# A hybrid decoder layer on one core: sliding-window scores and value products of two heads joined on halves of the TensorE array

## The chip, the cores and the metric

The kernel runs on one core of a Trainium2 chip. The metric is the device time of one execution in microseconds, as the median of repeated runs.

## The reference

One decoder layer over 2048 tokens of width 1024, all in float32. A mixer (four HGRN2 heads beside eight sliding-window query heads), then cross attention over 256 memory tokens, then an MLP. The change touches only the sliding-window group:

```
q: 8 heads x 64, k and v: 2 heads x 64 (4 query heads share one key head)
q, k = partial_rope(head_rms(.))           # per head
query block n (128 rows) reads key blocks n-1 and n (256 keys), causal, window 128
s = q k^T / 8;  m = max(max(s), sink);  p = exp(s - m)
o = (p / (sum(p) + exp(sink - m))) v       # (128 rows x 64) per head and block
```

## The kernel before

**Staging.** The mixer works through the sequence in four blocks of 512 tokens (`TB`), everything with the feature on the partitions and the token along the free axis. In each block, 22 projection panels (128 output features) are multiplied in three products of split operands (lines 1560, 1563 and 1570), each panel as the steps `("make", n, part)`, and each is copied out by ScalarE in the step `take`. Beside them run the HGRN2 heads 0 to 3 (`hg_...`, `gate_...`, `spans_...`) and the sliding attention of the head pairs t = 0 to 3.

**Order.** All engines follow one list of steps written out by hand (`mixer_steps`, woven by `weave` with `PLACES`): each engine issues its own part of a step, in the order of the list, and waits on semaphores (`Signal.at`). For the attention of a pair the list is made by `attend(t)`. A pair has two heads of 64 features that lie on partitions 0 to 63 and 64 to 127 of `qk`. It has four sub-steps q = 0 to 3, numbered through a block by a = 4t + q: q = 0 and 1 are the even and the odd head of query tiles 0 and 1, q = 2 and 3 the even and the odd head of tiles 2 and 3. The list runs them as a pipeline of four stages:

```
for n in range(QT + 3):
    scores(n);  scale(n-1) + turn(n-2);  pv(n-3)     # each if its number is 0 to 3
```

- `scores` (TensorE, line 1703): two matmuls of 128 queries by 256 keys into one of three banks. The stationary operand is all 128 partitions of `qk`, both heads; the other head's half of the moving `kpad` holds zeros. `kpad` has four planes: key head times even or odd. VectorE adds the window and takes the maximum (line 1502, into `s_sb`, three places), ScalarE takes the exponential (line 1244) and the sink's (line 1248).
- `scale` (VectorE, lines 1514 to 1519): the denominators, and two multiplications.
- `turn` (TensorE, line 1714): four transposes of 128x128 into the bank `TURN`; it waits until ScalarE has emptied `TURN` of the sub-step before. ScalarE copies `TURN` to `pT` (line 1256), which has two places.
- `pv` (TensorE, line 1726): four matmuls with the 128x64 values as stationary operand and 128 columns of `pT`, into the 64 partitions of the bank `OUT` that belong to the even or the odd head.

Behind the last `pv`, the step `hg_transpose` of the next head (lines 1612 and 1617) waits for the last copy of `TURN`, and `att_out` copies `OUT` (line 1262). The steps `hg_scores` (line 1643: seven levels, two output halves of 64 partitions in turn, 64 columns each) and `hg_delta` (line 1626: eight matmuls of 128 columns with 64 partitions of contraction each, the two halves of the partitions in turn, into two banks) belong to the HGRN2 heads.

**Keys.** `sw_keys` multiplies the rotated keys by duplicating matrices (lines 1690, 1691), and ScalarE copies them in four pieces of 64 partitions to the planes of `kpad` (line 1236); the rotation of the first pair (line 1686) waits for these copies, since it writes the bank `ROT`. VectorE moves the last key tile to the front for the next block (line 1458). `kpad` is cleared once, at the start (line 1327). The squares of the next block's norm use the first two places of `pT` as their buffer (`sq`).

Of the kernel before, what the change touches and what calls it, by code (L numbers as in the profile page):

```python
# [23 lines left out]
ACT = mybir.ActivationFunctionType  # L24
AX = mybir.AxisListType

P = 128
# [5 lines left out]
TB = 512  # L33
NBLK = SEQ // TB
QT = TB // P
# [722 lines left out]
def mixer(nc, block, sems, sh, xT, w_mix, rope_d, y_d, w_cross, lows_d):  # L758
# [17 lines left out]
    with ExitStack() as ctx:  # L776
# [45 lines left out]
        tn = sb("tn", [P, 2, TB])  # L822
        tcos = sb("tcos", [P, TB])
        qk = sb("qk", [P, 2, TB])
        kpad = sb("kpad", [P, 4, P + TB])
        vsw = sb("vsw", [P, 1 + QT, P])
        s_sb = sb("s_sb", [P, 3, 2, 2 * P])
        pT = sb("pT", [P, 2, TB])
        sq = pT
        stat = sb("stat", [P, 3, 5, 2])  # L830
        small = sb("small", [P, 3, 2 * QT])
# [238 lines left out]
        def _(act):  # L1070
# [80 lines left out]
            def turn(blk, steps):  # L1151
                for step in steps:
# [76 lines left out]
                    elif kind == "sw_keys":  # L1229
                        act.wait_ge(k_old.sem, k_old.at(blk, 0))  # L1230
                        for kv in range(2):
                            done = (k_dup0, k_dup1)[kv]
                            act.wait_ge(done.sem, done.at(blk, 0))
                            for n in range(2):
                                rows = slice(n * SW_D, (n + 1) * SW_D)
                                last = act.activation(kpad[rows, 2 * kv + n, P:], (TURN, ROT)[kv][rows, :], ACT.Copy)
                            last.then_inc((k_ok0, k_ok1)[kv].sem, 1)
                    elif kind == "scores":
                        a = step[1]
                        t, q = ATT[a]  # L1240
# [9 lines left out]
                    elif kind == "turn":  # L1250
                        a = step[1]
                        act.wait_ge(a_tr.sem, a_tr.at(blk, a))
                        act.wait_ge(a_o.sem, a_o.at(blk, a - 2))
                        if ATT[a][0] == 1 and has_next(blk):
                            act.wait_ge(n_sum.sem, n_sum.at(blk, KT - 1))
                        act.activation(pT[:, a % 2, :], TURN[:], ACT.Copy).then_inc(a_pt.sem, 1)
                    elif kind == "att_out":
                        t = step[1]
                        act.wait_ge(a_o.sem, a_o.at(blk, (t + 1) * QT - 1))
                        out = stored[3 if t == SW_PAIRS - 1 else 1]  # L1260
                        act.wait_ge(out.sem, out.at(blk, -1))
                        act.activation(yT[:, HEADS + t, :], OUT[:], ACT.Copy).then_inc(y_att.sem, 1)
                        if t == SW_PAIRS - 1:
                            out = block_of(y_d, blk)
                            act.wait_ge(y_hg.sem, y_hg.at(blk, HEADS - 1))
                            act.dma_start(out[:, HEADS - 1, :], yT[:, HEADS - 1, :]).then_inc(stored[2].sem, 16)
                            act.wait_ge(y_att.sem, y_att.at(blk, t))
                            act.dma_start(out[:, KT - 1, :], yT[:, KT - 1, :]).then_inc(stored[3].sem, 16)
# [11 lines left out]
        def _(dve):  # L1280
# [42 lines left out]
                                  ALU.mult).then_inc(p_ok.sem, 1)  # L1323

            dve.wait_ge(sh["kept"], 48)
            for t in (state[:], kpad[:], vsw[:, QT, :], vtok[:], rope[:, 1, :]):
                dve.memset(t, 0.0).then_inc(set_up, 1)
            dve.memset(rope[:, 0, :], 1.0).then_inc(set_up, 1)
            dve.wait_ge(set_up, 6)
# [1 line left out]
            def turn(blk, steps):  # L1331
                for step in steps:
# [118 lines left out]
                    elif kind == "sw_values":  # L1451
# [3 lines left out]
                        dve.wait_ge(v_ok.sem, v_ok.at(blk, -1))  # L1455
                        dve.tensor_copy(vsw[:, 0, :], vsw[:, QT, :]).then_inc(v_old.sem, 1)
                        dve.wait_ge(k_ok1.sem, k_ok1.at(blk, -1))
                        dve.tensor_copy(kpad[:, :, 0:P], kpad[:, :, TB:]).then_inc(k_old.sem, 1)
                    elif kind == "sw_root":

                        n = step[1]
# [68 lines left out]
        def _(pe):  # L1530
# [65 lines left out]
            def turn(blk, steps):  # L1596
                for step in steps:
# [94 lines left out]
                    elif kind == "scores":  # L1692
                        a = step[1]
                        t, q = ATT[a]
                        if q == 0:

                            pe.wait_ge(h_pr.sem, h_pr.at(blk, (t + 1) * NCH // 2 - 1))
                            pe.wait_ge(s_qk.sem, s_qk.at(blk, 1 + t))
                        if q >= 3:
                            pe.wait_ge(a_s.sem, a_s.at(blk, a - 3))  # L1700
                        for i in range(2):
                            tq = q // 2 * 2 + i
                            last = pe.matmul(SCORE[a % 3][:, i * 2 * P:(i + 1) * 2 * P],  # L1703
                                             qk[:, t % 2, tq * P:(tq + 1) * P],
                                             kpad[:, t // 2 * 2 + q % 2, tq * P:(tq + 2) * P], start=True, stop=True)
                        last.then_inc(a_sc.sem, 1)
                    elif kind == "turn":
                        a = step[1]
                        pe.wait_ge(a_pn.sem, a_pn.at(blk, a))
# [7 lines left out]
                    elif kind == "pv":  # L1717
                        a = step[1]
                        t, q = ATT[a]
                        if q == 0:  # L1720
                            pe.wait_ge(h_y.sem, h_y.at(blk, t))
                        pe.wait_ge(a_pt.sem, a_pt.at(blk, a))
                        for i in range(2):
                            tq = q // 2 * 2 + i
                            for kt in range(2):
                                last = pe.matmul(OUT[q % 2 * SW_D:(q % 2 + 1) * SW_D, tq * P:(tq + 1) * P],  # L1726
                                                 vsw[:, tq + kt, t // 2 * SW_D:(t // 2 + 1) * SW_D],
                                                 pT[:, a % 2, (2 * kt + i) * P:(2 * kt + i + 1) * P],
                                                 start=kt == 0, stop=kt == 1)
                        last.then_inc(a_o.sem, 1)  # L1730

            pe.wait_ge(s_xhi, KT)
            pe.wait_ge(s_xln, 4 + KT)
# [1606 lines left out]
```

## Time and profile before

| | |
|---|---|
| median of 3 runs | 2691.37 us (2687.94 to 2693.91) |
| the profiled execution's own time | 2685.68 us |
| its span from first to last instruction | 2683.9 us |
| TensorE busy | 2594.5 us, 97% |
| VectorE busy | 1731.4 us, 65% |
| ScalarE busy | 1145.2 us, 43% |
| the mixer | from about 84 to 976 us of the span |

Times are microseconds. A float32 matmul is recorded as two instructions. A matmul's recorded duration holds the time to fill and drain the array, so the pace of a group is read from the chain or from the starts, not from the mean. "[0.77 <-ACT ktok L1214]" means that the engine had been idle for 0.77 us and what ended it.

### The profile page before, as it was taken

How to read it: one execution, taken by the hardware profiler on the slowest of the kernel's cores; microseconds unless marked ns; L12 is line 12 of the kernel's file. 1: busy time of each engine (PE TensorE's matmuls, PEld its weight loads, DVE VectorE, ACT ScalarE, POOL GpSimd, SP SyncE). 2: the span in 40 equal slices, each digit the busy share in tenths (PEclk: the TensorE clock that was granted, in tenths of full speed). 3: DMA queues.
4: the chain of work that ended last, by engine and by line, in shares of the span. 5: the costliest groups of instructions: out<-in, count | busy, mean ns of one | idle time of the engine just before them, and what ended most of it. 6: DMA issues, size and time to landing. Idle time of an engine off the chain costs nothing.

```text
span 2683.9 us, 39324 instructions
## 1 busy us (share of the span) xinstructions
PE 2594.5 (97%) x13654; PEld 2110.1 (79%) x13654; DVE 1731.4 (65%) x3010; ACT 1145.2 (43%) x2179; POOL 896.4 (33%) x1018
## 2 busy tenths in 40 slices
PE   7999999999999989999998999999999999999999
PEld 5777777777777878877786888888888888888887
DVE  6678567756756656575657586687666354556665
ACT  5455455555445545654565332252223233332231
POOL 1332100000000037336535576747666222222222
PEclk9999999999999999999999999999999999999999
DMA  4432532343243343145315234423334963444664
GB/s 181 144 111 80 184 103 95 113 165 95 94 168 106 104 176 130 52 166 196 115 51 195 95 126 153 142 98 122 124 121 138 325 176 102 137 138 142 208 186 146
DMA packets 184509, 369.17 MB, mean 138 GB/s; under 512 B 13168, under 2 KB 79088, under 8 KB 181616
## 3 DMA queue, kind: packets, MB, share of 16 engines
q1 hardware_dynamic: 179152, 357.08, 39.9%
q10 hardware_dynamic: 5152, 9.51, 1.0%
q8 instruction: 110, 1.80, 0.3%
q14 instruction: 95, 0.78, 0.1%
HBM read 286.71 MB, written 79.82 MB: 137 GB/s over the span
## 4 chain that ended last, share of the span: by engine, by line
PE 78%; DVE 9%; ACT 5%; issue 4%; DMA 2%; POOL 2%; ACTq 0%; DVEq 0%; SPq 0%; POOLq 0%
PE bank L3256 8%; PE bank L3254 8%; PE bank L3258 8%; PE bank L3234 6%; PE bank L3230 6%; PE bank L3231 6%; PE bank L1570 5%; PE bank L1560 5%; PE bank L1563 5%; PE bank L2184 2%; PE bank L2179 2%; PE bank L2180 2%; PE bank L1726 2%; PE bank L1643 2%; PE bank L1703 2%
## 5 line engine op out<-in xcount | busy, mean ns | idle before, releaser
L478 POOL TENSOR_TENSOR wlo<-raw,whi 128x256 fp32r<-128x256 f32 x372 | 321.1, 894 | 1119.0 <-ACT whi L1162 641.9
L1560 PE MATMUL bank<-hi,whi 128*128 128x512 f32 x704 | 297.4, 422 | 2.0 <-ACT whi L1158 1.9
L1563 PE MATMUL bank<-lo,whi 128*128 128x512 f32 x704 | 279.9, 398 | 4.7 <-DVE lo L1314 4.7
L3256 PE MATMUL bank<-lo,whi 128*128 128x512 f32 x896 | 275.8, 389 | 0.0
L3254 PE MATMUL bank<-hi,whi 128*128 128x512 f32 x896 | 275.8, 389 | 0.0
L3258 PE MATMUL bank<-hi,wlo 128*128 128x512 f32 x896 | 275.8, 389 | 0.0
L3046 DVE TENSOR_TENSOR lo<-h,hi 128x1024 fp32r<-128x1024 f32 x80 | 124.5, 1556 | 172.8 <-ACT hi L2810 172.8
L2741 POOL TENSOR_TENSOR wlo<-h,whi 128x256 fp32r<-128x256 f32 x160 | 127.8, 823 | 298.3 <-ACT whi L2802 298.3
L2179 PE MATMUL bank<-hi,whi 128*128 128x512 f32 x504 | 208.6, 414 | 10.5 <-DVE h L2072 6.5
L2180 PE MATMUL bank<-lo,whi 128*128 128x512 f32 x504 | 197.8, 393 | 0.0
L3258 PEld LDWEIGHTS bank<-hi,wlo 128*128 128x128 f32 x896 | 168.2, 188 | 34.9
L3256 PEld LDWEIGHTS bank<-lo,whi 128*128 128x128 f32 x896 | 168.2, 188 | 34.9
L3254 PEld LDWEIGHTS bank<-hi,whi 128*128 128x128 f32 x896 | 168.2, 188 | 34.9
L2723 POOL TENSOR_TENSOR wlo<-raw,whi 128x256 fp32r<-128x256 f32 x166 | 151.1, 936 | 122.2 <-ACT whi L2751 120.0
L1570 PE MATMUL bank<-hi,wlo 128*128 128x512 f32 x704 | 189.9, 412 | 0.0
L2802 ACT ACTIVATE whi<-h 128x512 fp32r<-128x512 f32 x80 | 50.6, 632 | 289.1 <-PE bank L3258 271.4
L1563 PEld LDWEIGHTS bank<-lo,whi 128*128 128x128 f32 x704 | 134.3, 191 | 38.7 <-DVE lo L1314 9.4
L2723 POOL TENSOR_TENSOR m_xlo<-raw,m_xhi 128x256 fp32r<-128x256 f32 x174 | 163.6, 973 | 0.0
L1560 PEld LDWEIGHTS bank<-hi,whi 128*128 128x128 f32 x704 | 134.3, 191 | 34.7 <-issue 7.0
L1570 PEld LDWEIGHTS bank<-hi,wlo 128*128 128x128 f32 x704 | 130.8, 190 | 35.0 <-issue 9.6
L2751 ACT ACTIVATE whi<-raw 128x512 fp32r<-128x512 f32 x87 | 54.5, 629 | 228.2 <-DMA raw<-w_mlp 184.6
L3230 PE MATMUL bank<-hi,whi 128*128 128x512 f32 x348 | 136.0, 391 | 1.1 <-issue 0.6
(395 smaller groups left out, 5804.9 us busy)
## 6 DMA issues: line engine op xcount, KB each, us to landing
h<-hidden_scratch SPq DMA_DIRECT2D x96, 512.0 KB, 4.3
raw<-w_mix SPq DMA_DIRECT2D x88, 512.0 KB, 4.1
raw<-w_cross SPq DMA_DIRECT2D x64, 512.0 KB, 3.4
raw<-w_mlp SPq DMA_DIRECT2D x64, 512.0 KB, 4.6
wlo<-mixer_lows_scratch SPq DMA_DIRECT2D x60, 512.0 KB, 3.5
hidden_scratch<-hT SPq DMA_DIRECT2D x116, 256.0 KB, 2.0
h<-w_mlp SPq DMA_DIRECT2D x112, 256.0 KB, 3.0
mixer_lows_scratch<-wlo SPq DMA_DIRECT2D x22, 512.0 KB, 2.9
```

Source lines behind the costliest of these rows:

```text
L478: last = pool.tensor_tensor(wlo[:, i, cols], raw[:, i, cols], whi[:, i, cols].bitcast(F32), ALU.subtract)
L1560: pe.matmul(out, w, hi[:, k, :], start=k == 0, stop=False)
L1563: pe.matmul(out, w, lo[:, k, :], start=False, stop=False)
L1570: last = pe.matmul(out, wlo[:, i % 2, k * P:(k + 1) * P], hi[:, k, :], start=False, stop=k == KT - 1)
L2179: pe.matmul(out, w, hi[b][:, k, :], start=k == 0, stop=False)
L2180: pe.matmul(out, w, lo[b][:, k, :], start=False, stop=False)
L2723: last = pool.tensor_tensor(lo_tile[:, cols], source(half, n, w)[:, cols], hi_tile[:, cols].bitcast(F32), ALU.subtract)
L3230: pe.matmul(acc, hi_tile[:, cols], parts(half, m, k)[0], start=k == 0, stop=False)
L3231: pe.matmul(acc, hi_tile[:, cols], parts(half, m, k)[1], start=False, stop=False)
L3254: pe.matmul(down_bank(i)[:], wh[:, cols], xh[:, i % 2, :], start=K == 0, stop=False)
L3256: pe.matmul(down_bank(i)[:], wh[:, cols], xl[:, i % 2, :], start=False, stop=False)
L3258: last = pe.matmul(down_bank(i)[:], wl[:, cols], xh[:, i % 2, :], start=False, stop=K == KD - 1)
```

## The change

The two heads of a pair are computed together. `kpad` (four planes with zeros in one half) becomes `ksw` (two planes, both halves filled), copied by one 128-partition instruction for each key head. The score matmuls of q = 0 and 1, and those of q = 2 and 3, are issued together at the place of the even one, each with 64 partitions of contraction, and the even and odd head alternate. The value products of a pair of sub-steps are issued together at the place of the odd one, with the two output halves alternating. `pT` has four places, and the copy into it waits for the value product four sub-steps back.

```diff
-        kpad = sb("kpad", [P, 4, P + TB])
+        ksw = sb("ksw", [P, 2, P + TB])
-        pT = sb("pT", [P, 2, TB])
+        pT = sb("pT", [P, QT, TB])
...
-                            for n in range(2):
-                                rows = slice(n * SW_D, (n + 1) * SW_D)
-                                last = act.activation(kpad[rows, 2 * kv + n, P:], (TURN, ROT)[kv][rows, :], ACT.Copy)
-                            last.then_inc((k_ok0, k_ok1)[kv].sem, 1)
+                            act.activation(ksw[:, kv, P:], (TURN, ROT)[kv][:], ACT.Copy).then_inc((k_ok0, k_ok1)[kv].sem, 1)
...
-                        act.wait_ge(a_o.sem, a_o.at(blk, a - 2))
+                        act.wait_ge(a_o.sem, a_o.at(blk, a - QT))
-                        act.activation(pT[:, a % 2, :], TURN[:], ACT.Copy).then_inc(a_pt.sem, 1)
+                        act.activation(pT[:, a % QT, :], TURN[:], ACT.Copy).then_inc(a_pt.sem, 1)
...
-                        dve.tensor_copy(kpad[:, :, 0:P], kpad[:, :, TB:]).then_inc(k_old.sem, 1)
+                        dve.tensor_copy(ksw[:, :, 0:P], ksw[:, :, TB:]).then_inc(k_old.sem, 1)
...
                     elif kind == "scores":
+                        if q % 2:
+                            continue
                         if q == 0:
...
-                        if q >= 3:
-                            pe.wait_ge(a_s.sem, a_s.at(blk, a - 3))
+                        else:
+                            pe.wait_ge(a_s.sem, a_s.at(blk, a - 2))
                         for i in range(2):
-                            tq = q // 2 * 2 + i
-                            last = pe.matmul(SCORE[a % 3][:, i * 2 * P:(i + 1) * 2 * P],
-                                             qk[:, t % 2, tq * P:(tq + 1) * P],
-                                             kpad[:, t // 2 * 2 + q % 2, tq * P:(tq + 2) * P], start=True, stop=True)
-                        last.then_inc(a_sc.sem, 1)
+                            for odd in range(2):
+                                rows = slice(odd * SW_D, (odd + 1) * SW_D)
+                                last = pe.matmul(SCORE[(a + odd) % 3][:, i * 2 * P:(i + 1) * 2 * P],
+                                                 qk[rows, t % 2, (q + i) * P:(q + i + 1) * P],
+                                                 ksw[rows, t // 2, (q + i) * P:(q + i + 2) * P], start=True, stop=True)
+                                if i:
+                                    last.then_inc(a_sc.sem, 1)
...
                     elif kind == "pv":
-                        if q == 0:
+                        if q % 2 == 0:
+                            continue
+                        if q == 1:
                             pe.wait_ge(h_y.sem, h_y.at(blk, t))
                         pe.wait_ge(a_pt.sem, a_pt.at(blk, a))
-                        for i in range(2):
-                            tq = q // 2 * 2 + i
+                        for tq in (q - 1, q):
                             for kt in range(2):
-                                last = pe.matmul(OUT[q % 2 * SW_D:(q % 2 + 1) * SW_D, tq * P:(tq + 1) * P],
-                                                 vsw[:, tq + kt, t // 2 * SW_D:(t // 2 + 1) * SW_D],
-                                                 pT[:, a % 2, (2 * kt + i) * P:(2 * kt + i + 1) * P],
-                                                 start=kt == 0, stop=kt == 1)
-                        last.then_inc(a_o.sem, 1)
+                                for odd in range(2):
+                                    last = pe.matmul(OUT[odd * SW_D:(odd + 1) * SW_D, tq * P:(tq + 1) * P],
+                                                     vsw[:, tq + kt, t // 2 * SW_D:(t // 2 + 1) * SW_D],
+                                                     pT[:, q - 1 + odd, (2 * kt + tq - q + 1) * P:(2 * kt + tq - q + 2) * P],
+                                                     start=kt == 0, stop=kt == 1)
+                                    if tq == q and kt:
+                                        last.then_inc(a_o.sem, 1)
```

## Rows read from the trace of the kernel before

**Rows 1.** The page: the span, and part 1, busy time of each engine.

```profile
span 2683.9 us, 39324 instructions
PE 2594.5 (97%) x13654; PEld 2110.1 (79%) x13654; DVE 1731.4 (65%) x3010; ACT 1145.2 (43%) x2179; POOL 896.4 (33%) x1018
```

**Rows 2.** Stretch 84 to 976: PE, PEld, DVE, ACT, POOL busy; clock, DMA.

```profile
84.00:976.00 892.00, 852.97 (x5960) 685.60 (x5959) 599.94 (x1565) 465.97 (x1016) 75.78 (x96) 0.98 0.35 119
```

**Rows 3.** The chain that ended last, 84 to 976: shares by line.

```profile
by line: PE bank L1570 15.9%; PE bank L1560 14.7%; PE bank L1563 14.4%; PE bank L1726 6.1%; PE bank L1643 5.4%; issue 5.3%; PE bank L1703 5.2%; PE bank L1714 3.2%; PE bank L1656 2.4%; PE bank L1657 2.1%; DVE lo L1314 1.8%; PE bank L1686 1.6
```

**Rows 4.** Groups of TensorE instructions by line, 84 to 976.

```profile
L1703 PE MATMUL bank<-kpad,qk 128*128 128x256 f32 x256 | 65.9, 380 | 1.3 <-DVE qk L1491 1.3
L1726 PE MATMUL bank<-pT,vsw 128*64 128x128 f32 x511 | 64.2, 279 | 0.0
```

**Rows 5.** The chain in order of time (start, length), pair 0 of block 1.

```profile
367.32 0.87 PE bank L1703 x4
...
372.26 1.02 PE bank L1726 x8
373.28 0.43 PE bank L1560
...
373.94 0.24 PE bank L1560
...
379.26 1.77 PE bank L1726 x16
381.04 0.59 PE bank L1612 x4
```

**Rows 6.** The chain in order of time: `hg_scores` and `hg_delta` of head 2.

```profile
437.47 1.78 PE bank L1643 x56
...
443.11 1.09 PE bank L1626 x16
```

**Rows 7.** Timeline: the last `turn` of pair 0, and `hg_delta` of head 3.

```profile
378.66 0.60 PE L1714 MATMUL bank<-con,s_sb 128*128 128x128 f32 x4
...
379.30 0.60 ACT L1256 ACTIVATE pT<-bank 128x512 f32<-128x512 f32 x1 [2.29 <-PE bank L1714]
...
487.11 0.60 ACT L1214 ACTIVATE ktok<-bank 128x512 f32<-128x512 f32 x1
...
487.86 1.16 PE L1626 MATMUL bank<-vtok,ktok 64*128 64x128 f32 x16 [0.77 <-ACT ktok L1214]
```

**Rows 8.** Timeline: TensorE's wait in pair 1; pair 2 before its second `turn`.

```profile
413.04 1.10 PE L1536 MATMUL bank<-sqsum,con 128*128 128x512 f32 x2 [1.97 <-ACT nguess L1085]
...
475.42 0.58 ACT L1256 ACTIVATE pT<-bank 128x512 f32<-128x512 f32 x1
...
476.80 0.60 PE L1714 MATMUL bank<-con,s_sb 128*128 128x128 f32 x4
```

**Rows 9.** Timeline: the keys of block 1 and the first scores.

```profile
350.93 2.40 ACT L1236 ACTIVATE kpad<-bank 64x512 f32<-64x512 f32 x4
351.06 0.69 DVE L1286 TENSOR_TENSOR rstd<-rstd,mean 128x512 f32<-128x512 f32 x1 [3.83 <-ACT rstd L1114]
...
353.38 1.12 PE L1686 MATMUL bank<-tn,rotq 128*128 128x512 f32 x2 [1.14 <-ACT kpad L1236]
...
356.71 1.10 PE L1703 MATMUL bank<-kpad,qk 128*128 128x256 f32 x4 [0.37 <-DVE qk L1491]
```

**Rows 10.** Timeline: the clearing of `kpad`, and TensorE's first wait behind it.

```profile
58.02 2.19 DVE L1327 MEMSET kpad<- 128x2560 f32 x1 [0.48 <-ACT fg L1125]
...
80.64 1.08 PE L1617 MATMUL bank<-con,kend 128*128 128x128 f32 x4 [2.77 <-ACT qdec L1193]
```

**Rows 11.** Who waited for whom, 84 to 976: total, times, longest.

```profile
DVE prod L1438 <- PE bank L1643: 73.1, 29, 8.1
DVE s_sb L1502 <- PE bank L1703: 18.7, 13, 1.9
```

**Rows 12.** Two stretches, columns as in the stretch of Rows 2.

```profile
405.00:420.00 15.00, 13.04 (x55) 9.88 (x54) 12.50 (x36) 10.80 (x24) 0.00 (x0) 1.00 0.26 75
490.00:505.00 15.00, 12.18 (x90) 8.59 (x90) 11.81 (x26) 3.59 (x9) 0.00 (x0) 0.77 0.12 37
```

More of the change, by code:

```diff
@@ L1325, in _ @@
             dve.wait_ge(sh["kept"], 48)
-            for t in (state[:], kpad[:], vsw[:, QT, :], vtok[:], rope[:, 1, :]):
+            for t in (state[:], ksw[:], vsw[:, QT, :], vtok[:], rope[:, 1, :]):
                 dve.memset(t, 0.0).then_inc(set_up, 1)
```

## The prediction

> **What bounds the kernel now.** The page comes first: TensorE is busy for 97% of the span, the next engine for 65% [rows 1]. The change touches the mixer only, so the second view is the busy time of that stretch: of 892.0 us TensorE is busy for 853.0, VectorE for 599.9, ScalarE for 466.0 [rows 2]. TensorE leads there too, but 39 us of it are gaps, so time taken from TensorE may be lost again to the engines that fill its gaps. The third view, the chain that ended last, says how much of the two touched lines counts now: the score matmuls hold 5.2% and the value products 6.1% of the stretch [rows 3], that is 46 and 54 us. The trace has 256 and 511 records of them [rows 4], 4 to a score sub-step and 8 to a value sub-step, so 64 sub-steps of each (4 blocks, 16 in each). At the lengths read below they take 55 and 61 us; so more than eight tenths of both lie on the chain, and this is work whose removal should show.
>
> **Step 1: what one sub-step costs.** From the chain in order of time: a score sub-step takes 0.87 us for 4 records, a value sub-step that stands alone 1.02 us for 8, and the last two, which stand together, 1.77 us for 16 [rows 5]. A record with 256 columns thus costs 0.215 us, and by columns one of 128 costs 0.107 and one of 64 costs 0.054. Eight of 0.107 are 0.86: entering the 64-column layout costs 0.16. Leaving it also costs: the first projection matmul behind a value sub-step takes 0.43 us, the next 0.24 [rows 5], so 0.20.
>
> **Step 2: do halves of the array work at the same time?** The kernel has both kinds already. `hg_delta` issues 16 records of 128 columns with 64 partitions of contraction, the two row halves in turn: one after the other they would take 16 x 0.107 = 1.71 us, and the chain has 1.09 [rows 6]. `hg_scores` issues 56 records of 64 columns, the output halves in turn: 3.0 us one after the other, 1.78 on the chain [rows 6]. So both kinds overlap. How well is read off the same rows. If the two records of a float32 matmul follow each other on one half and only the second runs beside the other half's first, m matmuls that alternate take m + 1 record lengths, not 2m. That gives 9 x 0.107 = 0.96 for `hg_delta`; the measured 1.09 is this and 0.13 for entering. I use this count.
>
> **Step 3: scores.** Four matmuls of 256 columns alternate between row halves. Cost of a joined pair: 5 x 0.215 = 1.07, entering 0.13, leaving 0.20, together 1.40 us. It replaces 2 x 0.87 = 1.73, which had neither entry nor exit, since its layout was that of the neighbours. Saved: 0.33 a pair, 0.66 for the four sub-steps of a head pair. Bounds: complete overlap and no layout cost, 0.86 (0.87 saved); no overlap, 1.73 + 0.33 = 2.06 (0.33 lost). I take 1.40, as `hg_delta` is the same operation with half the columns. The even head's scores come out as soon as before (its second matmul ends after 4 record lengths), so VectorE's start on them isn't late; those of q = 1 and 3 come one step early, which removes part of the 18.7 us that VectorE waited for scores [rows 11]. I count nothing for that.
>
> The Trainium skill ("TensorE: Matmul & The Clock Gate", section "Measured speedup vs the span model") has a packed group last as long as one member plus about 4 ns for each further one. By that a joined pair would take about 0.87 + 0.33 = 1.20 and each pair would save 0.2 more, 6 us in all. The row of `hg_delta`, 1.09 where that rule would give 0.86 before layout cost, lies between the two.
>
> **Step 4: value products.** First pair (q = 0, 1): before, 2 x 1.02 with two exits of 0.20, 2.44 us. After: 16 records of 128 columns, the shape of `hg_delta`'s group, 1.09, and one exit: 1.29. Saved 1.15. Bounds: 2 x 0.43 + 0.16 = 1.02, and without overlap 1.71 + 0.16 = 1.87, both before the exit. Second pair (q = 2, 3): before, q = 2 was issued straight behind the last `turn` and hid ScalarE's copy of it. Now q = 2 is held back to q = 3, which needs that copy, and nothing stands between. What is queued behind the waiting instruction is `hg_transpose` of the next head and so `hg_scores`, for which VectorE waits anyway. The copy runs from 379.30 to 379.90 [rows 7]. From the end of such a copy to the end of a 16-record alternating group takes 1.31 us where `hg_delta` waits the same way (487.71 to 489.02) [rows 7]. So the group would end at 381.21; before, it ended at 381.04 [rows 5]. Lost: 0.17. The value products save 1.15 - 0.17 = 0.98 for each head pair.
>
> The other waits: the third and fourth `turn` wait for the copies of the second and third; between these a projection part remains, or 1.09 us stand in place of 1.02. In pair 2 the second `turn` starts at 476.80 while the copy it needs ended at 476.00 [rows 8]; the score saving ahead of it is 0.66, so 0.1 of the cover is left.
>
> **Step 5: where gains are swallowed.** In pair 1 of the blocks that have a next block, TensorE waits 1.97 us for the root of the next block's norm, right after the first scores [rows 8]. That chain runs through VectorE and ScalarE, so the first 0.33 of that head pair only lengthens this wait: 3 x 0.33 = 1.0 lost. Elsewhere the saving passes on: VectorE stands waiting for TensorE's `hg_scores` at the start of the heads, 73.1 us in 29 times [rows 11], so the next stretch moves up with TensorE.
>
> **Step 6: keys and set-up.** ScalarE's four copies of 2.40 us become two of some 1.2, and TensorE's wait of 1.14 us before the rotation goes. But VectorE works without a gap from 351.06 to the `qk` that releases the first scores at 356.71 [rows 9], and it was released by an earlier ScalarE result; the wait moves to the scores. Gain: 0, at most 1.1 x 4. VectorE's move of the key tile (half the elements) lies before its idle of 3.83 us [rows 9]: 0. Clearing half of the buffer takes 1.1 us less of 2.19 at the head of a VectorE chain for which TensorE then waits 2.77 us [rows 10]: 1.1 gained. The four places of `pT` loosen a wait and cost nothing. No DMA is added or moved.
>
> **Sum.** 16 head pairs x (0.66 + 0.98) = 26.2, less 1.0, plus 1.1: 26 us. The profiled execution took 2685.7 and would take 2660. The median of the runs stands 5.7 above the profiled one; against it the forecast is 2691.4 - 26 = 2665.
>
> **The rivals.**
> - *More than I count (0.13).* Halves overlap completely and the VectorE and ScalarE chains start earlier, because the odd scores come early and the keys are quicker: 32 x 0.2 and 4 x 1.1 more, 37 us saved, 2654. For it: VectorE's waits [rows 11]. Against it: the pace of `hg_delta`.
> - *VectorE and ScalarE become the bound inside the pairs (0.17).* With TensorE ahead of them, `turn` waits for `scale` or for the copy. The cover in pair 2 is 0.8 us [rows 8]. If pairs 1 to 3 keep only half of their 1.64, 12 x 0.82 = 10 is lost: 16 us saved, 2675.
> - *Column halves do not overlap for these products (0.05).* Then the first pair costs 1.87 + 0.20, saving 0.37 instead of 1.15, and the second, 0.78 longer than above, loses 0.95; with the scores' 0.66 a head pair gains 0.08, and the whole 16 x 0.08 - 1.0 + 1.1 = 1 us: 2690, no change that shows. `hg_scores` speaks against it [rows 6]. The Trainium skill (same page, "The mechanism") says that a weight load overlaps running matmuls only when the row group differs; here both column halves use all rows. By that rule this rival would hold; the 1.78 us of `hg_scores`, which also differs in columns alone, contradicts it.
> - *The clock falls (0.05), the rival on the other side.* From 490 to 505 TensorE was busy for 12.18 of 15 us and the granted clock was 0.77 of 2.4 GHz (it dropped to 1.2 GHz for part), which cost 3.4 us [rows 12]. If the new waits bring such a fall into every head pair, 16 x 3.4 = 55 is added: 2720. It decides from 26 / 3.4, eight of the sixteen. Against it: the stretch with the wait of 1.97 us, 13.04 of 15 busy, kept 1.00 [rows 12], and the new wait is under 1 us.
>
> **How the numbers follow.** My own case has 0.58, with 2657 to 2673 as its own range (score pairs between 1.20 and 1.60, a few tenths of new waits). The first two rivals, 0.13 and 0.17, are faster too: 0.88 in all. The column rival and 0.02 for nothing in particular give 0.07 within 0.2% (5 us, about what a measurement can tell); the clock gives 0.05 slower. The range of 2650 to 2680 takes in the first three cases but for their tails, 0.8.
>
> **What would show it.** The chain after should have a joined score group of 8 records at 1.2 to 1.4 us with 0.2 behind it, a first value group of 16 at about 1.1, and before the second one a TensorE wait of some 0.7 us for ScalarE's copy of `TURN`, 16 times. TensorE's wait on the `kpad` copies should be gone, and a longer one on `qk` should stand in its place. Wrong would be: score records spaced at 0.2 us (no overlap), new waits at `turn` of over 0.5 us, or a granted clock of the mixer under 0.98.

## The result, and the profile after

The changed kernel takes 2660.56 us (median of 4 executions, 2658.54 to 2663.62) against 2689.65 us (4, 2686.21 to 2693.91) for the kernel before, run on the same chip: ratio 0.9893, 95% interval 0.9878 to 0.9908. It is faster by 29 us; the forecast was 26 us and 2665. The profiled execution took 2658.5 us, 27 less than that of before.

The page of the changed kernel, the lines that answer to [rows 1]:

```profile
span 2656.7 us, 39316 instructions
...
PE 2548.2 (96%) x13654; PEld 2054.7 (77%) x13654; DVE 1731.6 (65%) x3010; ACT 1142.4 (43%) x2171; POOL 901.1 (34%) x1018
```

Since the mixer now starts and ends elsewhere, the stretch of [rows 2] is read again from the first `hg_scores` to the end of the mixer in each kernel, together with the 5 us ahead of it. Columns as in [rows 2]. The changed kernel:

```profile
81.80:949.00 867.20, 808.39 (x5957) 631.11 (x5958) 600.25 (x1565) 462.98 (x1009) 76.66 (x96) 0.98 0.36 122
...
79.00:84.00 5.00, 4.63 (x70) 3.93 (x71) 1.33 (x3) 3.81 (x7) 1.08 (x2) 1.00 0.45 129
```

And the kernel before, over its own stretch:

```profile
84.50:976.00 891.50, 852.47 (x5958) 685.46 (x5958) 599.94 (x1565) 465.87 (x1015) 75.47 (x96) 0.98 0.35 119
...
79.00:84.00 5.00, 3.36 (x11) 2.85 (x12) 1.45 (x6) 4.19 (x8) 0.00 (x0) 0.66 0.51 170
```

The stretch is 24.3 us shorter, and it starts 2.7 us earlier; together 27.0, the difference of the two profiled executions. In the stretch TensorE's busy time fell by 44.1 us (852.5 to 808.4), and its gaps rose by 19.8 (39.0 to 58.8). VectorE and ScalarE do what they did before. TensorE still leads with 93% of the stretch.

The chain in order of time (start, length), pair 0 of block 1, against [rows 5]:

```profile
354.76 1.06 PE bank L1703 x8
355.82 0.43 PE bank L1557
...
366.53 1.02 PE bank L1729 x16
367.55 2.05 PE bank L1567 x8
369.60 0.45 PE bank L1715 x4
370.07 0.61 ACT pT L1253
370.72 1.09 PE bank L1729 x16
371.82 0.59 PE bank L1609 x4
```

L1703 is the joined score group, 8 records in 1.06 us, and the matmul behind it takes 0.43, not 0.23: the exit of 0.20. L1729 is the joined value group, 16 records in 1.02 us where 8 records alone took 1.02. The second value group is the last but one line; the chain now goes through ScalarE's copy of `TURN` (L1253) ahead of it, where it passed over TensorE before. From the start of the last `turn` to the end of the values it takes 369.60 to 371.82 = 2.22 us. Before, the last `turn` started at 378.83 and the values ended at 381.04 [rows 5], 2.21 us:

```profile
378.83 0.44 PE bank L1714 x4
```

The groups of the two touched lines (busy, mean ns | idle before), against [rows 4], and the shares of the chain, against [rows 3]:

```profile
L1703 PE MATMUL bank<-ksw,qk 64*128 64x256 f32 x256 | 36.3, 402 | 6.6 <-DVE qk L1488 6.6
...
L1729 PE MATMUL bank<-pT,vsw 128*64 128x128 f32 x512 | 35.0, 279 | 11.0 <-ACT pT L1253 11.0
```

```profile
by line: PE bank L1567 15.8%; PE bank L1557 14.7%; PE bank L1560 14.1%; issue 6.0%; PE bank L1640 5.5%; PE bank L1729 3.5%; PE bank L1715 3.3%; PE bank L1703 3.1%; PE bank L1653 2.5%; PE bank L1654 2.2%; DVE lo L1311 1.8%; PE bank L1623 1.5
```

The busy time of scores fell from 65.9 to 36.3, that of values from 64.2 to 35.0, for the same number of records; on the chain they went from 5.2% and 6.1% to 3.1% and 3.5%.

Where the gaps grew: who waited for whom in 84 to 976 (total us, times, longest), the changed kernel:

```profile
PE bank L1729 <- ACT pT L1253: 11.0, 16, 0.7
PE bank L1653 <- DVE st L1427: 9.5, 4, 4.7
PE bank L1533 <- ACT nguess L1085: 7.2, 3, 2.4
PE bank L1533 <- ACT sqsum L1220: 7.0, 4, 1.8
PE bank L1703 <- DVE qk L1488: 6.6, 4, 1.8
PE bank L1560 <- DVE lo L1311: 5.4, 9, 1.1
PE bank L1715 <- ACT pT L1253: 4.8, 3, 1.7
...
PE bank L1715 <- DVE s_sb L1516: 1.8, 2, 0.9
```

The same waits of the kernel before:

```profile
PE bank L1656 <- DVE st L1430: 8.7, 4, 4.7
...
PE bank L1536 <- ACT nguess L1085: 5.9, 3, 2.0
...
PE bank L1686 <- ACT kpad L1236: 4.4, 4, 1.1
...
PE bank L1714 <- ACT pT L1256: 2.0, 3, 0.8
...
PE bank L1703 <- DVE qk L1491: 1.3, 3, 0.5
```

The first line of after is the forecast new wait: 16 times 0.69 us. The others are small lengthenings of waits that were there: `turn` for the copy of the earlier result (2.0 to 4.8), `turn` for the scaled scores `s_sb` (0 to 1.8), the root `nguess` (5.9 to 7.2), the keys (`qk` and `kpad` together 5.7, now `qk` alone 6.6), `st` (8.7 to 9.5), and `lo` (4.7 to 5.4, its line of before not shown). They are 8.3 us together, of the 8.8 by which the gaps grew beyond the 11.0.

The set-up (start, length, [idle before <- releaser]), against [rows 10]:

```profile
58.12 1.12 DVE L1324 MEMSET ksw<- 128x1280 f32 x1 [0.22 <-ACT fg L1125]
...
79.37 0.63 PE L1614 MATMUL bank<-con,kend 128*128 128x128 f32 x4 [1.90 <-ACT qdec L1193]
```

TensorE comes out of this wait 1.27 us earlier (80.64 to 79.37). The same four matmuls then take 0.63 us and not 1.08: the granted clock of 79 to 84 is 1.00, where it was 0.66 before. That is the other 1.4 of the 2.7 us. It belongs to this execution and not to the kernel: in e10, the changed kernel again, the wait is the same 1.90 us, the granted clock of 79 to 84 is 0.66, and the first `hg_scores` starts at 82.73 and not at 81.77.

### The profile page after: what moved, and what is told of

It is laid out like the page before. It is cut to its first block, busy times and chain, and to the rows that moved or that the text cites. A ratio compares the mean times of both kernels' runs of the same rounds, so it can differ in the third digit from the quotient of the medians.

```text
span 2656.7 us, 39316 instructions
## 1 busy us (share of the span) xinstructions
PE 2548.2 (96%) x13654; PEld 2054.7 (77%) x13654; DVE 1731.6 (65%) x3010; ACT 1142.4 (43%) x2171; POOL 901.1 (34%) x1018
## 4 chain that ended last, share of the span: by engine, by line
PE 69%; DVE 10%; issue 7%; POOL 5%; ACT 5%; DMA 2%; ACTq 0%; DVEq 0%; SPq 0%; POOLq 0%
PE bank L3260 8%; PE bank L3258 8%; PE bank L3262 8%; PE bank L1567 5%; PE bank L1557 5%; PE bank L1560 5%; PE bank L3238 4%; PE bank L3235 4%; PE bank L3234 4%; PE bank L2188 3%; PE bank L2183 3%; PE bank L2184 3%; POOL m_xlo L2727 2%; POOL wlo L2727 2%; PE bank L1640 2%
```

## The experiments

Diffs are against the changed kernel, but where noted. Ratios are against the kernel before, run on the same chip, with their 95% intervals.

**Each half alone.** e1 takes the joined scores and the unpadded keys, and issues the value products head by head, as before:

```diff
-                        for tq in (q - 1, q):
+                        for i in range(2):
+                            tq = q // 2 * 2 + i
                             for kt in range(2):
-                                for odd in range(2):
-                                    last = pe.matmul(OUT[odd * SW_D:(odd + 1) * SW_D, tq * P:(tq + 1) * P],
+                                last = pe.matmul(OUT[q % 2 * SW_D:(q % 2 + 1) * SW_D, tq * P:(tq + 1) * P],
...
```

> The score half alone: keys unpadded, scores of the two heads joined on row halves, four places for the turned probabilities, but each value product at its old place and in its old form. Theory A (the gain is the overlap of halves, each part by itself): a joined score group stays at 1.06 us with 0.20 us behind it instead of 1.73, 0.47 saved 32 times, 15 us on paper and 10 to 15 of it in the time: 2675 to 2680 against 2690 before. The TensorE wait for the last copy of the turned scores (11.0 us in 16 times in the changed kernel) is absent. Theory B (the value products carry the gain; 64-row groups cost what they save in entering and leaving the layout): within 3 us of before.

Measured: 2677.80 us (5 executions, 2676.24 to 2679.84), ratio 0.9953 (0.9940 to 0.9966): 12.9 us saved.

e2 is the kernel before, with padded keys and separate scores, and only the value products joined; its third place for turned probabilities is a buffer that is free there. Against the kernel before:

```diff
-                        act.wait_ge(a_o.sem, a_o.at(blk, a - 2))
+                        act.wait_ge(a_o.sem, a_o.at(blk, a - 3))
...
-                        for i in range(2):
-                            tq = q // 2 * 2 + i
+                        for tq in (q - 1, q):
                             for kt in range(2):
+                                for odd in range(2):
...
```

> The value half alone: padded keys and scores as before, value products of a pair of sub-steps joined on column halves. The turned probabilities have three places (a buffer of the rotation serves as the third, since four do not fit beside the padded keys). Theory A: first value group 2.44 to 1.22 us with its exits, second unchanged but for its wait: 1.2 us saved 16 times, 15 to 20 us in the time, 2670 to 2675; with the score half it adds up to the full change or somewhat more. Theory B of swallowed gains: each half alone keeps nearly all it saves on paper, and the sum of both is 5 us or more above what both together give, since both draw on the same slack of VectorE and ScalarE.

Measured: 2675.84 (5, 2674.40 to 2677.59), ratio 0.9947 (0.9934 to 0.9959): 14.8 us saved. The two halves give 27.7 together, the whole change 29. Each of the three is known to some 4 us, so within that they add up: that the halves take 5 us or more from each other is not seen.

**Does the order within a group matter?** e3 issues all eight value records of the even head, then all eight of the odd one:

```diff
-                        for tq in (q - 1, q):
-                            for kt in range(2):
-                                for odd in range(2):
+                        for odd in range(2):
+                            for tq in (q - 1, q):
+                                for kt in range(2):
```

> The full change, but in a joined value group all eight matmul halves of the even head come first, then those of the odd head: same work, same places, same waits. Theory A (column halves overlap only where they alternate): a group of 16 goes from 1.02 and 1.09 to about 1.7 us, 32 times 0.65: 17 to 21 us slower than the changed kernel, about 2680. Rival (the gain is from fewer entries into the 64-column layout and from the place, not from overlap): within 3 us of the changed kernel.

Measured: 2672.32 (6, 2666.99 to 2675.18), ratio 0.9934 (0.9922 to 0.9946), which lies clear above the changed kernel's. The difference of the ratios is 0.0041, 11 us, where 17 to 21 was expected. The chain of e3 says why:

```profile
424.11 1.51 PE bank L1729 x16
...
426.89 1.58 PE bank L1729 x16
```

The groups take 1.5 to 1.6 us, neither the 1.02 of the alternating group nor the 1.9 that two separate ones would take: the odd head's records still ran in part beside the even head's. The loss is smaller than expected by the same cause.

e4 does the same to the scores, whose group has four records of each head:

```diff
-                            for i in range(2):
-                                for odd in range(2):
+                            for odd in range(2):
+                                for i in range(2):
```

> The full change, but in a joined score group the even head's two matmuls come first, then the odd head's. Theory A (the first record of a matmul runs beside the last one of the other half's, so four alternating matmuls take 5 record lengths and four in two blocks take 7): a group goes from 1.06 to about 1.5 us, 32 times 0.43: 11 to 14 us slower than the changed kernel, about 2673. Rival (row halves are taken in whatever order and all overlap): no change.

Measured: 2660.99 (4, 2656.55 to 2664.08), ratio 0.9893 (0.9878 to 0.9908): the same as the changed kernel. The loss of 11 to 14 us that the count of step 2 makes here did not come. The chain of e4:

```profile
410.62 1.07 PE bank L1703 x8
```

So I read the starts of the single records in both traces. They come two by two:

```
             start of record, us
changed      410.333 .340 | .653 .660 | .869 .876 | 411.085 .092
e4           410.550 .563 | .870 .883 | 411.087 .100 | .302 .316
```

Within a pair the two starts are 7 ns apart (13 in e4 but for the last). From the first pair to the second it is 0.32 us, with half of the entry in it, and from there on 0.215, the length of one record. No half waits for the other: 4 x 0.215 = 0.86 us and 0.20 for the entry make 1.06. Records of one half can't start 13 ns apart if each takes it for 0.215 us, so in e4 an odd record must have started beside each even one, although all four even ones were issued first. In e3 the even head's first four records start alone (369.299, .459, .568, .677), and the odd head's first starts with the fifth (369.792 and .786). The last record of each head, which raises the semaphore, starts at 370.114 and 370.607; so the even head's eight follow each other at 0.109 us, and the odd head's run 0.49 us behind them.
**Is it the halves that save, or the shorter contraction?** e7 keeps the unpadded keys and takes every sub-step's scores by itself, in its old place, on 64 partitions:

```diff
-                        if q % 2:
-                            continue
...
+                        rows = slice(q % 2 * SW_D, (q % 2 + 1) * SW_D)
...
-                            for odd in range(2):
-                                rows = slice(odd * SW_D, (odd + 1) * SW_D)
...
```

> The full change, but the scores are not joined: each of the 64 score sub-steps stands at its old place, with 64 rows of its own head and no partner. Theory A (halves of the array gain only by running beside each other): a sub-step takes its old 0.86 us and 0.2 us for entering and 0.2 us for leaving the 64-row layout, 1.26 us where a joined pair takes as much: 64 x 1.26 - 32 x 1.26 = 40 us more TensorE time, 25 to 40 us slower than the changed kernel, 2686 to 2700, and 10 to 25 us slower than with padded keys and joined values. Rival (a matmul with 64 rows takes half the time by itself, which would explain why the order inside the joined group made no difference): a sub-step takes 0.43 + 0.2, as much for two as one joined group, and the whole lies within 8 us of the changed kernel.

Measured: 2687.68 (12, 2683.87 to 2694.58), ratio 0.9999 (0.9990 to 1.0009), 28 us above the changed kernel by the ratios, and 14 above e2, which joins the values and keeps the padded scores. Its chain:

```profile
358.03 1.06 PE bank L1701 x4
359.09 2.04 PE bank L1567 x8
```

Four records that are alone take as long as eight that are paired, and longer than the four padded ones before (0.87 [rows 5]), since each sub-step now enters and leaves the layout. Half a contraction alone saves nothing.

e8 keeps the joined order but puts both heads on the same half, so it computes the even head's scores twice and leaves the odd head's out:

```diff
-                                rows = slice(odd * SW_D, (odd + 1) * SW_D)
+                                rows = slice(0, SW_D)
```

> The full change, but both heads of a joined score group use the first 64 partitions of queries and keys, so the odd heads' scores are those of the even heads. Theory A (the two row halves work at the same time whatever the order of issue, within a few records of look-ahead): without the second half there is nothing to run beside, a group of 8 records takes 1.7 us and more in place of 1.06, 15 to 20 us slower than the changed kernel. Rival (64 rows take half the time by themselves): 1.06 us as before.

Measured, one execution: 2691.96, some 31 us above the changed kernel where 15 to 20 was expected. The chain has the group at 1.92, which is 8 x 0.215 and 0.20; 32 groups that are 0.86 longer are 27.5 us, and the expectation had taken 1.7 and left the entry out:

```profile
419.79 1.92 PE bank L1703 x8
421.71 2.07 PE bank L1567 x8
```

**The keys.** e6 copies the keys in 64-partition halves, so that ScalarE issues four copies as before:

```diff
-                            act.activation(ksw[:, kv, P:], (TURN, ROT)[kv][:], ACT.Copy).then_inc((k_ok0, k_ok1)[kv].sem, 1)
+                            for n in range(2):
+                                rows = slice(n * SW_D, (n + 1) * SW_D)
+                                last = act.activation(ksw[rows, kv, P:], (TURN, ROT)[kv][rows, :], ACT.Copy)
+                            last.then_inc((k_ok0, k_ok1)[kv].sem, 1)
```

> The full change, but ScalarE copies the keys in four pieces of 64 partitions again, into the unpadded buffer. Theory A (step 6: VectorE works without a gap to the first scores, the copies are beside it): no change, within 2 us of the changed kernel; in the trace the TensorE wait before the rotation (1.1 us a block) comes back and the one before the first scores shrinks by as much. Rival: the four copies lie on the path, 4 x 1.1 us slower.

Measured: 2661.58 (4, 2659.83 to 2663.65), ratio 0.9894 (0.9880 to 0.9908): no difference. The waits of e6 show the exchange, 4.5 ahead of the rotation and 0.9 ahead of the scores, against none and 6.6 in the changed kernel:

```profile
PE bank L1686 <- ACT ksw L1236: 4.5, 4, 1.1
...
PE bank L1706 <- DVE qk L1491: 0.9, 2, 0.5
```

**The new wait, filled.** e5 takes four of the eight steps of a head's last projection part out of their place and puts them between the last `turn` and the last value products, where TensorE waits for the copy; the panel's `take` moves behind them:

```diff
...
+            if ("make", n, 2) in s:
+                s[s.index(("make", n, 2))] = ("make", n, 3)
+        at = steps.index([("pv", h * QT - 2)])
+        return steps[:at] + [[("make", n, 4)], [("pv", h * QT - 2)], [("take", n)]] + steps[at + 1:]
...
-                    for k in range(KT):
+                    for k in {2: range(KT), 3: range(KT // 2), 4: range(KT // 2, KT)}[part]:
...
```

> The full change, and half of the last projection product beside each head pair (four of its eight matmuls with the low weights, 0.9 us) is moved from between the second and the third turn (or from behind the first value group) to between the last turn and the second value group, its copy-out behind it. Theory A (the 11.0 us that TensorE waits in 16 times for the last copy are now the cost of the joined form, and lie on the chain): the waits go, 16 x 0.7, less new waits of 0.1 to 0.3 us at the third turn, whose cover gets shorter: 6 to 12 us faster than the changed kernel, 2649 to 2655. Rival (the copy of ScalarE and the chain behind it set the pace there, so TensorE only waits elsewhere, at the next head): within 3 us of the changed kernel.

Measured: 2656.24 (5, 2653.85 to 2663.86), ratio 0.9884 (0.9869 to 0.9900), which can't be told from the changed kernel's; the 6 to 12 us expected did not come. The waits of e5:

```profile
PE bank L1639 <- ACT ktok L1227: 6.1, 4, 1.6
PE bank L1731 <- ACT pT L1266: 4.8, 3, 1.7
PE bank L1731 <- DVE s_sb L1529: 4.7, 4, 1.8
...
PE bank L1745 <- ACT pT L1266: 0.7, 1, 0.7
```

The wait at the value products is gone (11.0 to 0.7). But the work that fills it is missing earlier: `turn` waits 4.7 for the scaled scores, not 1.8, and `hg_delta`'s wait for `ktok` doubled from 3.0 to 6.1, as the moved `take` stands in ScalarE's queue ahead of that copy. Of 10.3 us removed 6 come back at these two.

e9 is e5 with both answered: five steps stay and three move, and the `take` of heads 1 to 3 goes behind `hg_transpose`. Of its diff, what e5 doesn't have:

```diff
+for _h in range(1, HEADS):
+    _take = ("take", MIX_PANELS.index(("sw_q", _h)))
+    MIX_STEPS.remove(_take)
+    MIX_STEPS.insert(MIX_STEPS.index(("hg_transpose", _h)) + 1, _take)
...
+                    for k in {2: range(KT), 3: range(5), 4: range(5, KT)}[part]:
...
```

> The run with the filler before the last values, with two edits: three of the eight matmuls are moved in place of four, so that the third turn keeps more cover, and ScalarE's copies of the moved projection panel (first three head pairs of a block) come behind the copies that the next head's first products wait for. Theory A (the rest of the filler's gain was eaten by 2.9 us more of waiting for the scaled probabilities at the third turn and 3.1 us more for the copied keys of the next head): both fall back, the wait for the last copy stays under 3 us in all, and the run is 2 to 5 us faster than the first filler and 6 to 10 us faster than the changed kernel on the same chip. Rival (these waits only changed place and the pace is VectorE's): no faster than the first filler.

e10 is the changed kernel again, on the chip of e9:

> The changed kernel itself, on the chip of the run beside it, as the measure for it: 2658 to 2664. By the theory that TensorE's clock falls behind a wait of some 2.4 us in one execution and not in the next, the executions spread over 4 to 7 us by steps of some 1.6 us, and the wait behind which it falls is that for the root of the next block's norm.

Measured: e9 2657.06 (4, 2654.01 to 2660.77), ratio 0.9878 (0.9854 to 0.9901); e10 2662.69 (4, 2661.60 to 2663.74), ratio 0.9898 (0.9877 to 0.9919). The intervals of the ratios overlap, the executions on that one chip don't: e9 is 5.6 us below, a little short of the 6 to 10 expected. It is faster than the kernel before by 33 us; whether it is faster than e5 too is not shown, as the intervals of the two overlap and they ran on different chips. The executions of e10 lie within 2.1 us, not the 4 to 7 expected. The waits of e9:

```profile
PE bank L1735 <- ACT pT L1270: 4.8, 3, 1.7
PE bank L1735 <- DVE s_sb L1533: 3.8, 3, 1.6
PE bank L1643 <- ACT ktok L1231: 3.0, 4, 0.8
PE bank L1660 <- DVE prod L1452: 2.3, 4, 0.6
```

The wait for `ktok` is at 3.0 again, `s_sb` has come down a little, and 2.3 us for `prod` are new. Part of the 5.5 us between the profiled executions (2656.4 and 2662.0) is the clock's, of which the next section tells: behind the root's wait alone it fell in two blocks of e9 and in three of e10. Where it stayed at 1.00 in both, in pairs 0 and 2 of block 1, e9 is shorter by 0.7 (65.84 against 66.52) and 0.6 us (45.37 against 46.01).

## Why the prediction was right, and where its terms were off

The direction and the size are right, and the range held. That the size came out to 1 us is luck: behind it stand two errors of opposite sign, 8 us too little saved on paper and 9 us too little swallowed.

*Step 1 (what a sub-step costs)* held: an exit of 0.20 is seen behind each joined group, and the entry, 0.16 from the value sub-steps, is 0.20 for scores.

*Step 2 (m matmuls that alternate take m + 1 record lengths)* is wrong. The halves run at the same time all through: the record starts show four pairs at 0.215 and no fifth length, and e4, whose order that count would make slower, is not. The 1.09 of `hg_delta`, from which I took the count, is 8 x 0.107 = 0.86 and an entry of 0.23; I had split the same number as 0.96 and 0.13. One row could not tell the two apart, and the bound "complete overlap" was the truth. The rule of the Trainium skill that I set beside it ("TensorE: Matmul & The Clock Gate", section "Measured speedup vs the span model") was nearer: one member's length and 4 ns for a further one, where the record starts have 7 ns. The estimate by it for a joined pair was 1.20, and 1.26 was measured; the rest is the entry, 0.20 for an assumed 0.13.

*Step 3 (scores)*, the term mis-sized by that count: 1.06 and 0.20 = 1.26 a pair for a forecast 1.40. Saved 0.47 for 0.33, over 32 pairs 15.0 us for 10.6. e1, with the set-up's gain in it, gave 12.9.

*Step 4 (value products).* The first pair costs 1.02 and 0.20 = 1.22 for a forecast 1.29: saved 1.22 for 1.15. The second: the wait of 0.69 us came, 16 times, as forecast, but it costs 0.0 and not 0.17: the group starts 0.05 us behind the copy's end (370.67 to 370.72) where `hg_delta` starts 0.15 behind it, and it takes 1.09 and not 1.16. So the second pair only breaks even, and the gain is the first pair's. Over 16 head pairs 19.5 us for 15.7; e2 gave 14.8.

*Step 5 (what is swallowed)* was far too small: 1.0 us at the root's wait, against 8.8 us of waits that grew beyond the copy's 11.0. They are the second rival in part, with its own sign seen: `turn` waits for the copy and for the scaled scores, 4.6 us more together, and the longest such wait, 1.7 us, is over the 0.5 that I had called wrong. The cover of 0.1 that I had left in pair 2 gave way in block 0 alone (1.7 for the copy, 0.9 for `s_sb`); the largest part, 3.1 us, stands in pair 3 of block 3. On paper 34.5 us were there to be had, and the stretch became shorter by 24.3.

*Step 6 (keys and set-up).* Keys at 0: right, e6 shows it both ways, and the wait moved to `qk` as said. The set-up gained 2.7 and not 1.1: 1.27 by the shorter chain, 1.4 by the clock, which didn't fall in this execution and did in e10's. The kernels with unpadded keys have their first `hg_scores` at 81.8 to 82.9, so 1.6 to 2.7 early; e2 with padded ones has it at 84.4, as before.

*The sum* then is 34.5 saved, 10.2 swallowed and 2.7 at the start, 27.0; I had 26.2, 1.0 and 1.1.

*The rivals.* More than I count: its mechanism is true (complete overlap), its time is not, since the waits took the surplus. VectorE and ScalarE the bound: true for some 5 to 9 us, as above. Column halves that don't overlap: refuted, the value group takes 1.02 and not 1.87. The rule of the Trainium skill beside it (same page, "The mechanism") doesn't hold for these products, whose halves differ in columns alone: in the group at 366.53 weight loads start at 366.512 and .519, while the matmul records of 366.459 and .466, each 0.323 us long, are running. The clock: it falls in places, before and after, but not at the wait I feared; the mixer's mean stayed 0.98. In the changed kernel and in e10 no fall starts within 9 us behind one of the new 0.69 us waits. The wait for the root, grown from 1.97 to 2.42 us, is followed by one in some blocks and not in others. In pair 1 of block 1 the changed kernel kept it (timeline, then the stretch):

```profile
403.82 1.10 PE L1533 MATMUL bank<-sqsum,con 128*128 128x512 f32 x2 [2.42 <-ACT nguess L1085]
```

```profile
395.00:410.00 15.00, 12.58 (x56) 9.06 (x56) 12.53 (x36) 10.94 (x24) 0.00 (x0) 1.00 0.23 72
```

And e1 at the same place, behind the same wait, did not:

```profile
409.34 1.90 PE L1533 MATMUL bank<-sqsum,con 128*128 128x512 f32 x2 [2.40 <-ACT nguess L1085]
```

```profile
400.00:415.00 15.00, 12.61 (x50) 8.68 (x51) 12.51 (x37) 10.41 (x23) 0.00 (x0) 0.89 0.15 39
```

Such a fall to the lower level costs 1.6 us. From `hg_scores` to `hg_scores`, pair 1 of blocks 0 to 2 takes in the changed kernel 52.11, 51.92 and 53.49 us, in e10, the same kernel, 53.55, 53.51 and 53.53. The longer wait is not shown to be the reason: e2 has the wait of 1.97 us as before, and the granted clock is 0.89 behind it in blocks 0 and 2 (180 to 195 and 634 to 649), which take 1.6 us more than block 1 does.

Nor is it the one place where executions of one kernel differ. Against the changed kernel's, e10's profiled execution (2661.95 against 2658.54) loses 1.0 us in the set-up, 3.0 in pair 1 of blocks 0 and 1, 1.7 in pair 0 of block 2 (granted 0.89 over 570 to 585, behind a wait of 1.67 us for `qk` that both have) and 0.8 behind the mixer, and it gains 2.9 in pair 3 of block 1.

The lengths by head of both kernels show where the gain stayed and where it didn't (us, `hg_scores` to the next, the last to the end of the mixer):

```
           head pair 0   1      2      3
before, block 1   68.79  53.57  47.83  58.49
after,  block 1   66.54  51.92  46.01  57.88
before, block 3   69.66  49.67  47.83  36.67
after,  block 3   66.17  47.57  45.72  36.90
```

In pairs 0 to 2 some two us arrive (1.6 to 3.5), about the 2.16 on paper. In pair 3 they arrive in block 2 (58.48 to 56.47), but in block 1 only 0.6 do, and in block 3 it became 0.2 longer. The traces show why.

In block 1 the clock has the larger part in it. The stretches of pair 3 before, in the changed kernel and in e10, with granted clocks of 0.94, 0.91 and 1.00:

```profile
485.30:543.70 58.40, 54.81 (x373) 43.83 (x372) 37.21 (x100) 28.48 (x64) 0.00 (x0) 0.94 0.38 129
...
472.50:530.40 57.90, 53.79 (x374) 41.69 (x372) 37.14 (x100) 28.73 (x64) 0.00 (x0) 0.91 0.37 126
...
476.70:531.60 54.90, 49.58 (x375) 38.87 (x374) 37.13 (x100) 28.60 (x64) 0.00 (x0) 1.00 0.39 133
```

In e10 the same kernel takes 54.95 us there, 2.9 less than in the changed kernel's own profile. By these two, 0.09 of granted clock cost 2.9 us; an estimate from that gives 1 us for the 0.03 by which the changed kernel's is under that of before, of the 1.5 us missing. In block 3 it is `turn`'s wait for the copy, before (939.6 to 976.4) and after (912.4 to 949.4), 1.9 us longer, which is nearly all of the 2.16:

```profile
PE bank L1714 <- ACT pT L1256: 1.2, 2, 0.8
...
PE bank L1715 <- ACT pT L1253: 3.1, 2, 1.6
```

What stays open: how much of the 10.2 us swallowed is the waits' and how much the clock's, since I did not take the waits away one by one and no profiled execution is free of falls; and what decides whether the clock falls behind one and the same wait.

## What to carry to other kernels

Two groups of small matmuls that use different halves of the array, by rows or by columns, cost here as much as one; it is worth putting them next to each other. Where that makes the second wait for its input, compare the two: here the group became 0.68 us shorter (1.77 to 1.09) and waited 0.69, so it broke even. Count the entry and the exit of the layout, 0.2 us each here, once for a group, and make groups long. And where one engine is busy for 95% and two others feed it, take the waits that its shorter work will uncover as a term of the sum: here a quarter to a third of the paper gain went there, spread over six waits of which none was large.

## What the runs showed of the hardware

- The overlap of halves is complete: starts 7 ns apart and 0.215 us from pair to pair, for row halves (scores), the first step apart; for column halves (values) 7 ns and 0.109 us, and 16 records take 1.02 us, 0.86 and 0.16.
- It asks for both halves, not for short contraction: four records of 64 partitions alone 1.06 us, eight on both halves 1.06, eight on one half 1.92.
- TensorE doesn't need the halves to alternate in the program when the groups are short: with four records of each half the order makes no difference (e4), with eight it costs half a microsecond a group (e3, 1.51 for 1.02). The Trainium skill ("TensorE: Matmul & The Clock Gate", section "The mechanism") has matmuls start and end strictly in the order of the program; the starts of e3 and e4 say that this doesn't hold between halves.
- The granted clock behind one and the same wait of 2.4 us is 1.00 in one execution and falls to the lower level in another. The same holds behind the 1.90 us wait of the set-up (1.00 in the changed kernel's profile, 0.66 in e10's), and behind waits of 1.97 us it fell in two blocks of e2 and in none of the kernel before.
